# Six norms whose mean is made on all partitions at once: two 512-column products in place of column products, roots, and transposes

## The reference

```python
h = x
h = h + 0.5 * swiglu(rms_norm(h, ffn1_norm), w_gate, w_up, w_down)       # up1, down1
u = rms_norm(h, mix_norm) @ w_in                                          # in1
...                                                                       # attention and pooling, out1
h = h + 0.5 * swiglu(rms_norm(h, ffn2_norm), w_gate, w_up, w_down)       # up2, down2
x = rms_norm(h, final_norm)
# second block, twice: mixer (in2, out2; in3, out3) and convolving FFN (up3, down3; up4, down4)
y = rms_norm_2(h, nw[0]); y = mixer(y); h = h + rms_norm_2(y, nw[1])
y = conv_ffn(rms_norm_2(h, nw[2]), w_up, conv_w, conv_b, w_down); h = h + rms_norm_2(y, nw[3])

def rms_norm_2(x, w):
    return x * lax.rsqrt(jnp.mean(x * x, axis=-1, keepdims=True) + EPS) * w
```

## Time and profile before

| | |
|---|---|
| median of 3 runs | 2080.83 us (2079.55 to 2081.73) |
| the profiled execution: time | 2080.45 us |
| the profiled execution: span, first to last instruction | 2078.7 us |
| PE busy | 2064.1 us, 99% of the span |
| DVE, ACT, POOL busy | 1182.5, 761.2, 125.0 us |
| granted PE clock | nine tenths or more in each of 40 slices |

### The profile page before, as it was taken

How to read it: one execution, slowest core, us unless ns; L and a number is a source line. 1 busy time by engine, 2 the same in 40 slices (tenths; PEclk the granted TensorE clock), 3 DMA queues, 4 the chain that set the end, 5 groups by cost and what they waited for, 6 DMA issues and landing times.

```text
span 2078.7 us, 27218 instructions
## 1 busy us (share of the span) xinstructions
PE 2064.1 (99%) x10386; PEld 1693.2 (81%) x10386; DVE 1182.5 (57%) x1927; ACT 761.2 (37%) x1163; POOL 125.0 (6%) x137
## 2 busy tenths in 40 slices
PE   9999999999999999999999999999999999999999
PEld 8888888777888888988788888888876688888887
DVE  5444433776444433487778666633658877666433
ACT  5222222254322222463454322222557753223222
POOL 0000000400000000000002000000413220000001
PEclk9999999999999999999999999999999999999999
DMA  8323233312222222321121222233347732222222
GB/s 257 127 89 101 76 98 109 127 42 92 91 101 101 96 70 97 117 102 62 66 80 64 101 101 95 72 99 104 117 110 167 159 92 102 101 101 92 74 97 82
DMA packets 77790, 209.41 MB, mean 101 GB/s; under 512 B 46481, under 2 KB 49857, under 8 KB 61329
## 3 DMA queue, kind: packets, MB, share of 16 engines
q1 hardware_dynamic: 72384, 182.41, 27.7%
q0 software_dynamic: 2992, 12.45, 2.2%
q10 hardware_dynamic: 2336, 13.52, 2.0%
HBM read 195.22 MB, written 7.38 MB: 97 GB/s over the span
## 4 chain that ended last, share of the span: by engine, by line
PE 91%; DVE 5%; ACT 3%; issue 1%; POOL 1%; ACTq 0%; DVEq 0%
PE ps L1152 29%; PE ps L1154 28%; PE ps L1153 28%; ACT weigh L559 2%; DVE w_lo L1605 1%; PE ps L664 1%; PE ps L681 1%; DVE weigh L574 1%; DVE halves L581 1%; PE ps L649 1%; ACT w_hi L1597 1%; DVE weigh L591 1%; PE ps L752 0%; PE ps L1129 0%; ACT x_split L1683 0%
## 5 line engine op out<-in xcount | busy, mean ns | idle before, releaser
L1152 PE MATMUL ps<-x_split,w_hi 128*128 128x512 f32 (+1 forms) x1774 | 700.1, 395 | 0.0
L1154 PE MATMUL ps<-x_split,w_lo 128*128 128x512 f32 (+1 forms) x1774 | 687.7, 388 | 0.0
L1153 PE MATMUL ps<-x_split,w_hi 128*128 128x512 f32 (+1 forms) x1774 | 687.4, 387 | 0.0
L1587 ACT ACTIVATE w_hi<-raw 128x2048 fp32r<-128x2048 f32 (+3 forms) x144 | 242.2, 1682 | 494.5 <-PE ps L1154 491.1
L1152 PEld LDWEIGHTS ps<-x_split,w_hi 128*128 128x128 f32 x1774 | 333.1, 188 | 78.7 <-issue 12.3
L1615 DVE TENSOR_TENSOR w_lo<-raw,w_hi 128x2048 fp32r<-128x2048 f32 (+3 forms) x144 | 287.9, 1999 | 179.7 <-ACT w_hi L1587 179.2
L1154 PEld LDWEIGHTS ps<-x_split,w_lo 128*128 128x128 f32 x1774 | 333.1, 188 | 69.1
L1153 PEld LDWEIGHTS ps<-x_split,w_hi 128*128 128x128 f32 x1774 | 333.3, 188 | 67.9 <-issue 2.6
L1152 PE MATMUL ps<-act,w_hi 128*128 128x512 f32 (+1 forms) x1026 | 376.0, 367 | 1.9 <-DVE w_lo L1605 1.5
L1154 PE MATMUL ps<-act,w_lo 128*128 128x512 f32 (+1 forms) x1026 | 371.8, 362 | 0.0
L1153 PE MATMUL ps<-act,w_hi 128*128 128x512 f32 (+1 forms) x1026 | 371.7, 362 | 0.0
(11 more groups left out here) (249 smaller groups left out, 1783.4 us busy)
## 6 DMA issues: line engine op xcount, KB each, us to landing
raw<-in_w_up SPq DMA_DIRECT2D x87, 1024.0 KB, 4.9
raw<-in_w_down SPq DMA_DIRECT2D x29, 768.0 KB, 4.2
raw<-in_w_in SPq DMA_DIRECT2D x20, 1024.0 KB, 4.9
raw<-in_w_down SPq DMA_DIRECT2D x29, 640.0 KB, 3.9
raw<-in_w_out SPq DMA_DIRECT2D x8, 1024.0 KB, 4.9
raw<-in_w_in ACTq DMA_DIRECT2D x8, 1024.0 KB, 5.4
skew<-scratch POOLq DMA_DIRECT2D x1, 5120.0 KB, 33.7
biases<-skew POOLq DMA_DIRECT2D x16, 256.0 KB, 4.1
```

Source lines behind the costliest of these rows:

```text
L1152: pe.matmul(own, hi, rhs_hi, start=start, stop=False)
L1153: pe.matmul(own, hi, rhs_lo, start=False, stop=False)
L1154: return pe.matmul(own, lo, rhs_hi, start=False, stop=stop)
L1587: eng.activation(w_hi[:, w], raw[:, w], ACT.Copy).then_inc(hi_rounded, 1)
```

## The change

Six of the seven deferred norms (all but in3's, whose `inv4` is also used as a column) are made in another way:

1. ACT, `round_sum`: `ssum` rounded to float32r, 128x512, into the first half of `sum_parts`.
2. DVE, `rest_sum`: the rest, 128x512, into the second half.
3. PE, `wide_mean`: two matmuls with `mean_r` (all 1/1024, float32r, 128x128) as weights and the two parts as moving data, 512 columns each: bank 4 holds each token's mean on all partitions.
4. ACT, `wide_root`: square root of 128x512 into `rstd`.
5. DVE, `wide_inverse`: reciprocal of 128x512, in place in `rstd`.

The four column matmuls, the four transposes, the reciprocal of four columns and the copy are gone. `sum_parts` lies where `sq` lies. `mean_r` is made once by ACT. The unused third of the constants is no longer loaded.

```diff
+            def wide_mean(r):
+                pe.wait_ge(mean_rounded, 1)
+                pe.wait_ge(sum_lo, WIDE_MEANS.index(r) + 1)
+                pe.matmul(bank(STATS_BANK), mean_r[:, :], chunk(sum_parts, 0), start=True, stop=False)
+                pe.matmul(bank(STATS_BANK), mean_r[:, :], chunk(sum_parts, 1), start=False, stop=True).then_inc(ms_ready, 1)
...
-                mean_at, spread_at = ((6, 10), (MEAN_AT, SPREAD_AT))[a]
+                mean_at = (7, 27)[a]
...
                     if g == mean_at:
-                        mean_squares(st.stat)
-                    if g == spread_at:
-                        spread_roots(st.stat)
+                        wide_mean(st.stat)
...
-                    stats_at = 2 if st.name == "up2" else 5
+                    stats_at = 4 if st.name == "up2" else 6
...
                                     if k == stats_at:
-                                        mean_squares(st.stat)
-                                    if k == stats_at + 2:
-                                        spread_roots(st.stat)
+                                        wide_mean(st.stat)
...
+            def round_sum(r):
+                eng.wait_ge(ssum_ready, KD * (r + 1))
+                eng.activation(chunk(sum_parts, 0), ssum[:, :], ACT.Copy).then_inc(sum_hi, 1)
+            def wide_root(r):
+                eng.wait_ge(ms_ready, r + 1)
+                eng.activation(rstd[:, :], bank(STATS_BANK), ACT.Sqrt, bias=lbs[:, 31:32]).then_inc(std_ready, 1)
...
-                        if g == (7, 26)[a]:
-                            root(st.stat)
+                        if g == (1, 21)[a]:
+                            round_sum(st.stat)
+                        if g == (7, 27)[a]:
+                            wide_root(st.stat)
...
                     round_weights(eng, st.q0 + 2, 0, 0)
-                    root(st.stat)
+                    round_sum(st.stat)
+                    wide_root(st.stat)
...
+            def rest_sum(r):
+                eng.wait_ge(sum_hi, WIDE_MEANS.index(r) + 1)
+                eng.tensor_tensor(chunk(sum_parts, 1), ssum[:, :], chunk(sum_parts, 0).bitcast(F32), ALU.subtract).then_inc(sum_lo, 1)
+            def wide_inverse(r):
+                eng.wait_ge(std_ready, r + 1)
+                eng.reciprocal(rstd[:, :], rstd[:, :]).then_inc(inv_ready, 1)
+                eng.wait_ge(inv_ready, r + 1)
...
                     rest_weights(eng, st.q0 + 2, 0, 0)
-                    inverse(st.stat)
-                    eng.tensor_copy(rstd[:, :], bank(STATS_BANK)).then_inc(rstd_ready, 1)
+                    rest_sum(st.stat)
+                    wide_inverse(st.stat)
```

More of the change, by code:

```diff
@@ L209, in build @@
         vec = new("vec", NVEC)
-        small = new("small", 3 * P)
+        small = new("small", 2 * P)
+        mean_r = new("mean_r", P, F32R)
         lbs = new("lbs", 32)
@@ L216, in build @@
         ctx.enter_context(nc.sbuf_tensor("arena", [P, arena_words], F32))
-        ident, mean_d, mean_head = small[:, 0:P], small[:, P:2 * P], small[:, 2 * P:3 * P]
+        ident, mean_d = small[:, 0:P], small[:, P:2 * P]
         proj = at("proj", [P, 24 * T], F32, act_at)
@@ L273, in build @@
         small_landed = sem("small_landed")
+        mean_rounded = sem("mean_rounded")
         warm_clear = sem("warm_clear")
@@ L304, in build @@
         ssum_ready = sem("ssum_ready")
+        sum_hi = sem("sum_hi")
+        sum_lo = sem("sum_lo")
         ms_ready = sem("ms_ready")
@@ L386, in build, with spreads_up_to @@
         IN, OUT = ("in1", "in2"), ("out1", "out2")
+        WIDE_MEANS, SPREADS = (0, 1, 2, 4, 6, 10), (3, 5, 7, 8, 9, 11)
+        sum_parts = at("sum_parts", [P, 2 * T], F32R, sq_at)
+        def spreads_up_to(r):
+            return sum(n <= r for n in SPREADS)
         def key_bias(n, lo, nk):
@@ L1368, in second_pair_waits @@
                     pe.wait_ge(lo_rounded, st.q0 + 2)
-            MEAN_AT, SPREAD_AT = 26, 30
             VALUE_MEAN_AT, VALUE_SPREAD_AT = 38, 41
@@ L1802, in _ @@
                     round_x(eng, 0, m, COL["ffn1_norm"])
+            eng.wait_ge(small_landed, 16)
+            eng.activation(mean_r[:, :], mean_d, ACT.Copy).then_inc(mean_rounded, 1)
             eng.wait_ge(raw_landed[1], 16)
@@ L2015, in scale_half @@
                     if hf:
-                        eng.wait_ge(spread, st.stat + 1)
+                        eng.wait_ge(spread, spreads_up_to(st.stat))
                     else:
@@ L2229, in _ @@
                     for g in range(1, end + 1):
-                        if a and g == 26:
-                            eng.wait_ge(std_ready, st.stat + 1)
-                            eng.reciprocal(inv4, std4).then_inc(inv_ready, 1)
+                        if g == (1, 21)[a]:
+                            rest_sum(st.stat)
                         if g == (8, 31)[a]:
                             if a == 0:
-                                eng.wait_ge(std_ready, st.stat + 1)
-                                eng.reciprocal(inv4, std4).then_inc(inv_ready, 1)
                                 eng.wait_ge(sink_landed, 16)
@@ L2241, in _ @@
                                 link(eng.memset(csum[:, 0:PAD + 1], 0.0))
-                            eng.wait_ge(spread, st.stat + 1)
-                            eng.tensor_copy(rstd[:, :], bank(STATS_BANK)).then_inc(rstd_ready, 1)
-                            eng.wait_ge(rstd_ready, (2, 4)[a])
+                            wide_inverse(st.stat)
                         if a and g == 34:
@@ L2313, in _ @@
                         if g == 43:
-                            eng.wait_ge(spread, st.stat + 1)
+                            eng.wait_ge(spread, spreads_up_to(st.stat))
                             eng.tensor_copy(rstd[:, :], bank(STATS_BANK)).then_inc(rstd_ready, 1)
-                            eng.wait_ge(rstd_ready, 6)
+                            eng.wait_ge(rstd_ready, 1)
                         if g % KD == 0 and g > st.lead:
@@ L2339, in _ @@
                     rest_weights(eng, st.q0 + 2, 0, 0)
-                    inverse(st.stat)
-                    eng.tensor_copy(rstd[:, :], bank(STATS_BANK)).then_inc(rstd_ready, 1)
-                    eng.wait_ge(rstd_ready, ("up1", "in1", "up2", "in2", "up3", "in3", "up4").index(st.name) + 1)
+                    rest_sum(st.stat)
+                    wide_inverse(st.stat)
                 if st.evac in ("add", "hold"):
@@ L2583, in shape_constants @@
     tab = np.broadcast_to(tab.reshape(1, -1), (P, 4 * TAIL))
-    small = np.concatenate([eye, np.full((P, P), 1.0 / D, np.float32), np.full((P, P), 1.0 / P, np.float32)], axis=1)
+    small = np.concatenate([eye, np.full((P, P), 1.0 / D, np.float32)], axis=1)
     return {"mixer_consts": np.stack(mixers), "pool_tab": tab, "small_consts": small}
```

## The result

| | before | after |
|---|---|---|
| median | 2080.86 us (10 runs, 2079.55 to 2081.73) | 2086.24 us (10 runs, 2084.57 to 2087.41) |
| the profiled execution: time, span | 2080.45, 2078.7 us | 2086.09, 2084.3 us |
| PE, DVE, ACT busy | 2064.1, 1182.5, 761.2 us | 2063.4, 1200.0, 766.4 us |

The ratio is 1.0027 (1.0018 to 1.0035): the changed kernel is slower, by 5.4 us. That is inside the range on record (2079.5 to 2088.0), above 2085.0, where the forecast's own range ended, and twice the loss that the sum gave (+2.7).

The account below looks back on a forecast made before the run. PE, busy 99% of the span, was taken as the bound. Savings and waits at the six norms summed to +2.7 us on the profiled 2080.45, giving a median of 2083.5 us; range 2079.5 to 2088.0, the forecast's own 2080.5 to 2085.

Parts of the forecast that it names:

- rival 2: Reciprocal in the norms slower than read, 8 ns a column, 4.24 us: +6.9 us, 2087.7; chance 0.25.
- Within 0.2%: Whole kernel's time not to be told from no change, between 2076.7 and 2085.0 us; chance 0.62.
- What PE is spared: At each of six norms, two matmuls replace column products and transposes: PE spared 0.9 us each, 5.3 in all.
- The waits for the sum: PE waits for DVE's rest of the sum at the mean: 1.2 us in up1, 2.2 in in1, none elsewhere.
- R: Time of DVE's 512-column reciprocal in each norm: taken as 3.2 us, with ends 0.69 and 5.3.
- Rival 1: Reciprocal in the norms is an ordinary operation of 0.69 us: -2.0 us, 2078.8; chance 0.12.
- What R does: Later evacuations or weights: PE waits 0.65 us each in up3 and up4, 1.0 in in1, 2.4 in in2; none in up1, up2.
- the 1.0 us for POOL: In in1 the later evacuation delays the chain over DVE and POOL: PE waits 1.0 us more.
- Rival 4: Clock falls in in1's wait; 24 matmuls at 1.2 GHz add 5.5 us to +2.7: 2089.0; chance 0.07.

Follow-up runs that it names:

- kernel 1: Changed kernel with nine unused matmuls put ahead of PE's wait for the sum in in1, to fill that pause; 2086.4 us, ratio 1.0025.
- kernel 2: Changed kernel with unused matmuls filling both long PE pauses, nine in in1 and ten ahead of pair 3's weights in in2; 2083.98 us, ratio 1.0013.
- 4: The changed kernel run again as it is, on the chip of three other follow-up kernels; 2086.69 us, ratio 1.0026.
- 6: Changed kernel with root and reciprocal replaced by logarithm and exponential on ACT; 2080.26 us, ratio 0.9997.
- kernel 7: Kernel before with the new norms ahead of up1 and up2 alone, up1's mean one step later, behind k = 7; 2078.91 us, ratio 0.9988.
- 3: Changed kernel with in1's sum (ACT's rounding, DVE's rest) made ahead of pair 1's weights; 2085.76 us, ratio 1.0024.
- 5: Changed kernel with the six norms' reciprocal replaced by an ordinary maximum of the same shape; 2078.39 us, ratio 0.9989.
- 8: Logarithm and exponential on ACT, plus in1's sum ahead of weights, up1's mean behind k = 7, in2's root later in ACT's order; 2076.99 us, ratio 0.9982.

## Why the prediction was right, and where it was short

The direction is right, the waits stand at the places that were named, and the time is in the range. That it is in the range is in part luck: the range went to 2088.0 for rival 2, a reciprocal of 8 ns a column, and rival 2 is wrong. The measured 2086.2 us lie where it would have put them by another cause. "Within 0.2%" had 0.62, and the result is slower by 0.27%, which had 0.33.

- **What PE is spared**, 0.9 us a norm: right. The two new matmuls take 0.47 us (531.96 to 532.43 in up2), and up2, where nothing waits, came out at 0.91.
- **The waits for the sum**, 1.2 and 2.2 us: 0.92 and 2.13 as listed, 1.07 and 2.29 from start to start. None at the other four, as forecast.
- **R**, 3.2 us: 3.35, or (3352 - 146)/512 = 6.3 ns a column against the 6 taken from two rows of one line. This was the choice between 0.69 and 5.3 on which 4 of 6 terms hung. Rival 1 (0.69) and rival 2 (4.24) are out. So is the rate that an estimate from the Trainium skill, VectorE: DVE Perf Modes, section "First, the fixed hardware budget", gave with eight passes of 1.04 ns: 4.4 us.
- **What R does**: a listed wait of 2.41 us in in2 (2.4 forecast) and 0.74 each in up3 and up4 (0.65), nothing in up1 and up2. Without a fall in2 cost +1.57 (+1.5 forecast). up3 and up4 were each 0.36 us short in the sum (+0.11 against -0.25): 0.15 of it is R; and a wait listed with 0.74 cost PE 1.0, since to the 0.16 above comes a first matmul that holds the next one back (0.30 instead of 0.23 us). In in1 the 1.0 us for POOL is not in the first profiled execution, because slow matmuls had made PE late already; where the clock held (1, 2, 4) it is 1.0, and in1 cost 2.63 to 2.73 (+2.3 forecast).
- **The step that was short** is the clock. The sum had no term for it. Rival 4 had the mechanism in the right place but gave it 0.07, one place, and 24 matmuls. Measured were eight matmuls, 1.6 us a fall, and a second place, in2, where the prediction's own wait of 2.4 us was longer than the one that it thought of. In in2 all of it counts; in in1 it lies over the wait for POOL and 0.5 is left. This is shown three ways: by kernel 2, where only the pauses are filled, by in2 in kernel 1 against the changed kernel, and for in1 by the changed kernel's two executions.
- **Not from the change**: the wait for `x_split` ahead of up3 is 1.62 us before and 1.03 in all kernels but 6. It is 1.03 in kernel 7 too, where in2 is as before and PE comes earlier, not later. So the 0.3 us that it gave are no consequence of the new norms; why it has two lengths is open.

What stays open: what decides whether the clock falls after a pause. Pauses of 2.13 us were followed by a fall in one execution and not in the next, and one of 2.42 had none in kernel 1. Also open is why the executions of kernel 1 with and without falls lie 2.9 us apart. Not tried was an in1 whose chain over POOL itself is shorter.

## What to carry to other kernels

Price an operation that the trace doesn't show by two sizes of the same operation, down to its nanoseconds per column, and not by its neighbours of the same size. When a wait of PE of about two microseconds comes out of the sum, give the slow matmuls behind it a term: here eight, 1.6 us, behind five of eight such waits in the traces. And before a wait is taken away, ask what the chain behind it waits for: in in1 neither filling the pause of 2.1 us (1, 2) nor removing it (3) moved the next meeting with POOL by more than 1 us, and only a shorter chain (5, 8) took in1 under 2.6 us.

## What was not expected of the hardware

- The granted clock fell to 0.5 behind pauses of PE of 2.13 and 2.41 us, at the first matmul or about 1 us behind it, and not in every execution. In the kernel before, a pause of 1.62 us had no fall in its trace.
- A float32 reciprocal of 128x512 took 3.35 us and one of 128x4 0.17: five times an ordinary operation of 512 columns, and nothing to notice on four.
- Logarithm and exponential each had a load of their table ahead of them in every norm, 1.28 us each, so that the way over ACT cost 2.6 us behind the mean where its two operations took 1.3; the load ahead of the logarithm lay before the mean and cost nothing there.
